# In the first MLP product, 512-column and 256-column products alternate instead of standing two and two

## The reference, cut to what matters

```
h2 = rms_norm(x, g_mlp[layer])                       # 256 x 2048
x = x + jnp.square(jax.nn.relu(h2 @ w_mlp_in[layer])) @ w_mlp_out[layer]
                      # w_mlp_in 2048 x 8192, w_mlp_out 8192 x 2048
```

## Time and profile before

| | |
|---|---|
| median of 3 runs | 1630.17 us (1629.72 to 1630.33) |
| the profiled execution's own time | 1630.46 us |
| its span in the trace | 1628.6 us |
| TensorE matmul (PE) busy | 1616.6 us, 99% |
| TensorE weight load (PEld) busy | 1361.0 us, 84% |
| VectorE (DVE) busy | 1215.4 us, 75% |
| ScalarE (ACT) busy | 898.4 us, 55% |
| products of lines 1608 and 1612 | 1024 each |

### The profile page before, as it was taken

How to read it: one execution, slowest core, us unless ns; L and a number is a source line. 1 busy time by engine, 2 the same in 40 slices (tenths; PEclk the granted TensorE clock), 3 DMA queues, 4 the chain that set the end, 5 groups by cost and what they waited for, 6 DMA issues and landing times.

```text
span 1628.6 us, 20399 instructions
## 1 busy us (share of the span) xinstructions
PE 1616.6 (99%) x7974; PEld 1361.0 (84%) x7974; DVE 1215.4 (75%) x1470; ACT 898.4 (55%) x1248; POOL 79.0 (5%) x67
## 2 busy tenths in 40 slices
PE   9999999999999999999999999999999999999998
PEld 7888888888888888888888888888888888888886
DVE  7887778877666677766565567996699768986793
ACT  6666656766565445554444555654565455555562
POOL 3000000000000134000000000000000000000000
PEclk9999999999999999999999999999999999999999
DMA  7666665666556664445565775457635863576461
GB/s 270 193 207 201 187 188 188 206 195 205 174 186 185 190 186 154 143 143 179 182 234 193 259 235 190 157 206 235 190 125 202 273 190 130 207 262 189 144 233 52
DMA packets 134192, 312.19 MB, mean 192 GB/s; under 512 B 9744, under 2 KB 10448, under 8 KB 133968
## 3 DMA queue, kind: packets, MB, share of 16 engines
q1 hardware_dynamic: 129376, 302.21, 56.8%
q10 hardware_dynamic: 4720, 8.68, 2.1%
HBM read 308.68 MB, written 2.16 MB: 191 GB/s over the span
## 4 chain that ended last, share of the span: by engine, by line
PE 87%; DVE 9%; issue 2%; DMA 1%; ACT 1%; POOL 0%; POOLq 0%; ACTq 0%; DVEq 0%
PE G L1599 18%; PE G L1600 17%; PE G L1601 17%; PE S L1608 7%; PE G L1608 7%; PE G L1612 4%; PE S L1612 4%; PE S L1599 3%; PE S L1601 3%; PE S L1600 3%; DVE wlo L951 3%; DVE wlo_late L951 2%; PE S L1620 1%; DMA raw<-in_w_in 1%; DVE raw L954 1%
## 5 line engine op out<-in xcount | busy, mean ns | idle before, releaser
L602 ACT ACTIVATE whi<-raw 128x1024 fp32r<-128x1024 f32 x377 | 398.4, 1060 | 395.7 <-PE G L1601 317.0
L951 DVE TENSOR_TENSOR wlo<-raw,whi 128x1024 fp32r<-128x1024 f32 x377 | 461.0, 1236 | 133.6 <-ACT whi L602 132.8
L1599 PE MATMUL G<-whi,a_both 128*128 128x512 f32 x960 | 376.8, 393 | 2.2 <-DVE wlo L951 2.2
L1601 PE MATMUL G<-whi,a_both 128*128 128x512 f32 x960 | 373.8, 389 | 0.0
L1600 PE MATMUL G<-wlo,a_both 128*128 128x512 f32 x960 | 373.8, 389 | 0.0
L1599 PEld LDWEIGHTS G<-whi,a_both 128*128 128x128 f32 x960 | 180.3, 188 | 39.9 <-issue 2.8
L1601 PEld LDWEIGHTS G<-whi,a_both 128*128 128x128 f32 x960 | 180.2, 188 | 37.8
L1600 PEld LDWEIGHTS G<-wlo,a_both 128*128 128x128 f32 x960 | 180.4, 188 | 35.7
L1599 PE MATMUL G<-whi,b_hi 128*128 128x512 f32 x328 | 128.5, 392 | 0.3
L1600 PE MATMUL G<-wlo,b_hi 128*128 128x512 f32 x328 | 128.0, 390 | 0.0
L1601 PE MATMUL G<-whi,b_lo 128*128 128x512 f32 x328 | 127.7, 389 | 0.0
(11 more groups left out here) (283 smaller groups left out, 2591.7 us busy)
## 6 DMA issues: line engine op xcount, KB each, us to landing
raw<-in_w_in SPq DMA_DIRECT2D x208, 512.0 KB, 4.1
raw<-in_w_mlp_in SPq DMA_DIRECT2D x64, 512.0 KB, 4.3
gates<-in_w_mlp_in SPq DMA_DIRECT2D x64, 512.0 KB, 3.7
raw<-in_w_mlp_out SPq DMA_DIRECT2D x64, 512.0 KB, 4.9
gates<-in_w_mlp_out SPq DMA_DIRECT2D x64, 512.0 KB, 4.9
raw<-in_w_ssm_up SPq DMA_DIRECT2D x32, 512.0 KB, 3.6
raw<-in_w_attn_up SPq DMA_DIRECT2D x32, 512.0 KB, 4.0
raw<-in_w_out SPq DMA_DIRECT2D x32, 512.0 KB, 4.6
```

The lines of the kernel that those rows point to most:

```text
L602: act.activation(high(m), piece(n), ACT.Copy).then_inc(hi_made, 1)
L951: dve.tensor_tensor(low(m), piece(n), high(m).bitcast(F32), ALU.subtract).then_inc(lo_made, 1)
L1599: pe.matmul(out_ap, hi[:, k, cols], w_hi, start=start, stop=False)
L1601: return pe.matmul(out_ap, lo[:, k, cols], w_hi, start=False, stop=stop)
```

## The change

In each block the product of 256 columns for a k tile is issued right behind the product of 512 columns for the same k tile: 512, 256, 512, 256. The `start` and `stop` flags stay with the same products, and the instruction that adds to `used` is still the 256-column product of kk 1 in block 3.

```diff
             for c in range(4):
-                cols = [slice(kk * N + c * P, kk * N + (c + 1) * P) for kk in range(2)]
                 for kk in range(2):
-                    pe.matmul(banks[:, c, :], high(m)[:, cols[kk]],
-                              a_both[:, 2 * p + kk, :, :].rearrange("p h t -> p (h t)"),
-                              start=(p + kk == 0), stop=False)
-                for kk in range(2):
-                    last = pe.matmul(banks[:, c, 0:T], low(m)[:, cols[kk]], a_hi[:, 2 * p + kk, :],
-                                     start=False, stop=(2 * p + kk == KT - 1))
+                    cols, k = slice(kk * N + c * P, kk * N + (c + 1) * P), 2 * p + kk
+                    pe.matmul(banks[:, c, :], high(m)[:, cols], a_both[:, k, :, :].rearrange("p h t -> p (h t)"),
+                              start=(k == 0), stop=False)
+                    last = pe.matmul(banks[:, c, 0:T], low(m)[:, cols], a_hi[:, k, :], start=False, stop=(k == KT - 1))
             return last
```

## The result

The changed kernel takes 1635.29 us (median of 7 runs, 1635.08 to 1635.70), the kernel before 1630.22 in the same runs. The ratio is 1.0032, with a 95% interval of 1.0022 to 1.0042: slower, by more than the 0.2% that a measurement can tell. Forecast were 1630.2 us and no difference, with a range from 1625 to 1635.

What follows compares the result with a forecast made beforehand. TensorE's products bound the kernel, through the distance between their starts. The three terms (neighbours, cover of loads, order's surcharge) were each 0, so the median of 1630.17 us stayed: forecast 1630.2 us, range 1625 to 1635.

Steps and rivals of the forecast that it cites:

- What bounds the kernel, and how much each nanosecond weighs: TensorE's products are 87% of the span; every nanosecond between starts reaches the end; 512 quads (a block's four products), 356.7 us.
- First, the neighbours: In each quad, width changes go from two to four; with each product at its present price, 697 ns either way: change 0.
- The high bound of 706 ns: Dearest price of the new quad, longs at 235 ns and shorts at 118: 9 ns more each, 4.6 us in all.
- Second, what lies over the weight loads: In each quad, two loads start under shorts and two under longs in both orders, so change 0.
- Third, the order's own surcharge: A quad takes 697 ns against 680 from three unbroken-stream longs; put down to the shorts' price, not to order.
- the 17 ns: What each quad of the kernel before takes, 697 ns, beyond 680, three widths of a 226.7 ns long.
- My corrected 118 to 124: A short's full price in ns, with what is paid afterwards; it makes a quad 689 to 701 ns.
- the debt behind a run: Seven longs behind a run of six shorts still owe 33 ns, some 5 or 6 for each short.
- A: Faster: a single short between longs is absorbed; the whole 17 ns a quad gives 8.7 us less, 1621.5 us; chance 0.20.
- B: Slower: each width change in a quad costs 8.5 ns, 8.7 us more, 1638.9 us; visible from 3.2 ns; chance 0.18.
- C: TensorE gains but the splitters on VectorE and ScalarE don't follow, so 1630 again; chance next to nothing on its own.

Runs made afterwards that it cites:

- runs8: All eight 512-column products (longs) of a piece, then its eight 256-column ones (shorts), against the kernel before with two and two: 1630.89 us, ratio 1.0005.
- runs4: Four 512-column products of two blocks, then their four 256-column ones, against the kernel before with two and two: 1632.97 us, ratio 1.0015.
- pair_384: The kernel before's order, two and two, with the 256-column products widened to 384 columns: 826 ns for the four products of a block (a quad).
- alt_384: The changed kernel's alternating order with the 256-column products widened to 384 columns: 816 ns for the four products of a block.
- alt_long64: The changed kernel with the 512-column products' loads cut from 128 to 64 weight columns, but for the first k tile: 682 ns a quad.

## Why the prediction was wrong

*What bounds the kernel, and how much each nanosecond weighs:* right. 512 quads x 9.9 ns = 5.1 us, and the time rose by 5.1. The rest of the span, the waits and the clock (0.999 before, 0.998 after) did not move by more than 0.5 us and 0.001.

*"First, the neighbours. [...] With each kind of product at the price it has now, the sum does not move":* this is the step that failed. Its term in the sum was 0 and measured 9.9 ns a quad. A product does not keep its price when its neighbours change: longs went from 233.1 to 236.3 and shorts from 115.2 to 117.0. I had bounded the new quad by 680 and 706 and then took the value of the nearest rows, on the ground that they had the same four instructions. But the rows near it showed already that the four instructions do not fix the sum: the same long costs 227 in a stream and up to 235 behind shorts. The high bound of 706 ns was good: it gives 1634.8 us, my range ended at 1635, and the measured 706.9 ns and 1635.3 us lie just beyond both.

*"Second, what lies over the weight loads":* the count was right, two loads under shorts in both orders, one ahead in both. The conclusion, that the loads add nothing to the change, was not. In the alternating order the loads' width moves the quad by 25 ns (682 to 707), and not only the loads under the shorts do it (13 ns with the others halved); in the order two and two, halving all of them moves it by 2 ns the other way (697.0 to 699.1).

*"Third, the order's own surcharge":* the 17 ns were measured against a wrong base, half of a long, 113.3. By runs8 a short in a stream takes 120, so a clean quad is 693.3. My corrected 118 to 124 holds that; what failed is what I drew from it, that the price has "no term that asks about the order". Such a term is there: 3.7 ns of the quad before, and 13.6 in the changed one. The kernel before shows the 120 too, in another run of six shorts, whose single distances are 114, 119, 120, 120, 120 and 120 ns; its last four take 0.48 us:

```profile
73.83 0.28 PE L1601 MATMUL S<-xd_hi,bt_lo 128*128 128x256 f32 x1
...
74.31 0.40 PE L1599 MATMUL G<-whi,a_both 128*128 128x512 f32 x1
```

What I called the debt behind a run is seen again in runs8, 27 ns over the first five longs.

*The rivals.* A (a single short is absorbed) is refuted with full loads. It is what happens with half loads under the shorts: 682 ns in the alternating order, where two and two takes 700. B (each width change costs) had the sign, and its threshold of 3.2 ns a change was passed: 9.9 ns for two more changes are 5 each. The sign of it that I had named, longs to 236 and over, is there in the mean (236.3). Its mechanism is refuted all the same: runs4 and runs8 have fewer changes than the kernel before and cost more, and pair_384 has half the changes of alt_384 and costs 10 ns more. At 448 columns two changes less save only 2 ns, not 10. Its chance of 0.18 was too low for an arrangement that no row showed. C did not come up: TensorE got slower, and the splitters had more time.

*What is shown and what is open.* Shown: all of the loss is the distance between the products' starts; it hangs on order, on the width of the loads and on the width of the products together; it does not hang on the bank or on the weights' buffer, it does not follow the number of width changes, and it stays where the shorts take 175 to 178 ns (384 columns) and where they take 204 to 205 (448), more than the load's record of 188 ns. The single distances settle in short cycles: after the change 236 + 113, 233 + 117, 241 + 120 over and over, before it two quads by turns, such as 232, 231, 113, 119 and 234, 236, 115, 113. That looks like products and loads falling into step with each other, and it would fit that halving the loads helps one order and not the other. But it is only argued: no run took the mechanism apart, and I can't tell from it what a new order would cost. Not tested is the moving operand: alternating, a short reads the columns of `a_both` that the long just before it has read, and two and two it doesn't. That alone can't cost, since with half loads it is the cheap order, but no run separates it from the order with full loads. So the cause of the 9.9 ns stays open; shown is that order, load width and product width set them together.

## What to carry to other kernels

In a stream of TensorE products with a load each, don't price a new order with the distances of the old one: with TensorE busy 99% of the span, the same four instructions in another order cost from 697 to 707 ns, and on 512 repeats that was 5 us. Take the distance between starts, get the clean price from streams of one width (here columns / 2.4 + 13.3 ns), and expect, with full loads, some 1 to 7 ns a product on top where widths are mixed, with a sign between two orders that must be measured. Where no row shows the new pattern and everything rides on it, the bounds of its price are the forecast and the middle is not.

## What the runs showed of the hardware that I had not expected

- The fixed part of a product in a stream with full loads is 13.3 ns at three widths: 226.7 at 512 columns, 173.3 at 384, 120 at 256. At 128 columns it is not (109 ns in the transposes).
- With loads of 64 columns under the shorts, the alternating order gets below that (alt_long64): 682 ns a quad, 10.5 ns a product.
- Less work can take longer: halving the loads of either kind in the order two and two made a quad 2.7 to 6.5 ns dearer (699.7 and 703.5 against 697.0).
- The cost of an order changes sign with the width: alternating against two and two is +10 ns at 256 columns, -10 at 384 and +2 at 448, and -17 at 256 with all loads of 64 columns.
